# Logits in three fp32r passes, all query blocks per pair of heads, and probabilities scaled on GpSimd, in the sparse attention of a hybrid decoder layer

## The reference

```python
def block(args):                       # 128 queries each; here the kernel has its own blocks
    idx_logits = jnp.einsum('bqhd,bsd->bqhs', iqb, ik) * (IDX_HD ** -0.5)
    score = jnp.einsum('bqh,bqhs->bqs', iwb, jax.nn.relu(idx_logits))
    score = jnp.where(visible[None], score, -jnp.inf)
    _, idx = lax.top_k(score, k_sel)   # k_sel = 128 keys of 528
    ks, vs = k[idx], v[idx]
    logits = jnp.einsum('bqhd,bqkhd->bhqk', qb, ks) * (DSA_HD ** -0.5)
    logits = jnp.where(valid[:, None], logits, -jnp.inf)
    p = jax.nn.softmax(logits, axis=-1)
    return jnp.einsum('bhqk,bqkhd->bqhd', p, vs)
```

## Time and profile before

| | |
|---|---|
| median of 3 runs | 1045.75 us (1045.68 to 1053.85) |
| profiled execution: span, first to last instruction | 1044.6 us (no time of its own beside the span is given) |
| the runs' median above that span | 1.15 us |
| TensorE busy | 1033.1 us, 99% |
| VectorE busy | 782.0 us, 75% |
| GpSimd busy | 659.5 us, 63% |
| ScalarE busy | 471.6 us, 45% |
| granted TensorE clock, mean | 0.997 |
| instructions | 20236 |

### The profile page before, as it was taken

The page is one execution under the profiler, slowest core; times in us unless marked ns, Lnnn a source line. Parts: engine busy times, 40 slices in busy tenths (PEclk is TensorE's granted clock), DMA queues, the critical chain, the costliest instruction groups (busy, mean ns, idle before and its releaser), DMA issues.

```text
span 1044.6 us, 20236 instructions
## 1 busy us (share of the span) xinstructions
PE 1033.1 (99%) x7723; PEld 958.0 (92%) x7723; DVE 782.0 (75%) x1271; ACT 471.6 (45%) x766; POOL 659.5 (63%) x751
## 2 busy tenths in 40 slices
PE   9999999999999999999999999999999999999997
PEld 8999999999999999889878787778899999999997
DVE  7647897677676588699875584578999977777835
ACT  6433444334343354562455527444444443443335
POOL 6956787787686367269821304456887877866840
PEclk9999999999999999999999999999999999999999
DMA  7333342333432444345311102222333434334322
GB/s 209 101 98 97 97 112 82 112 96 97 111 94 80 122 118 116 83 117 149 90 33 41 42 21 63 79 71 81 84 101 103 122 107 112 101 92 111 92 61 81
DMA packets 178403, 98.73 MB, mean 95 GB/s; under 512 B 6787, under 2 KB 175798, under 8 KB 178310
## 3 DMA queue, kind: packets, MB, share of 16 engines
q1 hardware_dynamic: 178208, 97.38, 33.3%
q10 hardware_dynamic: 102, 0.08, 0.0%
HBM read 91.18 MB, written 2.10 MB: 89 GB/s over the span
## 4 chain that ended last, share of the span: by engine, by line
PE 93%; DVE 2%; ACT 1%; issue 1%; POOL 1%; DMA 1%; SPq 0%; DVEq 0%; ACTq 0%; POOLq 0%
PE ps L2542 44%; PE ps L2762 34%; PE ps L610 4%; PE ps L2578 2%; PE ps L799 1%; PE ps L748 1%; PE ps L778 1%; PE ps L916 1%; DMA xin<-in_x 1%; PE ps L957 0%; POOL wl L1852 0%; PE ps L691 0%; DVE mask L1404 0%; PE ps L811 0%; PE ps L595 0%
## 5 line engine op out<-in xcount | busy, mean ns | idle before, releaser
L1852 POOL TENSOR_TENSOR wl<-raw,wh 128x256 fp32r<-128x256 f32 x292 | 250.5, 892 | 198.6 <-ACT wh L1981 162.6
L1852 POOL TENSOR_TENSOR wxl<-raw,wxh 128x256 fp32r<-128x256 f32 x240 | 231.3, 989 | 140.5 <-ACT wxh L1981 140.0
L2542 PE MATMUL ps<-ah,wxh 128*128 128x264 f32 (+2 forms) x464 | 123.2, 319 | 0.3 <-POOL wxl L1852 0.3
L2542 PE MATMUL ps<-ah,wxl 128*128 128x264 f32 (+2 forms) x464 | 123.0, 318 | 0.0
L2542 PE MATMUL ps<-al,wxh 128*128 128x264 f32 (+2 forms) x464 | 122.8, 318 | 0.0
L2542 PE MATMUL ps<-xh,wh 128*128 128x264 f32 (+3 forms) x432 | 121.6, 333 | 0.2 <-DVE pja L1498 0.2
L2542 PE MATMUL ps<-xh,wl 128*128 128x264 f32 (+3 forms) x432 | 117.5, 323 | 0.0
L2542 PE MATMUL ps<-xl,wh 128*128 128x264 f32 (+3 forms) x432 | 117.4, 323 | 0.0
L2762 PE MATMUL ps<-xh,wh 128*128 128x264 f32 (+1 forms) x360 | 102.0, 283 | 0.0
L2762 PE MATMUL ps<-xl,wh 128*128 128x264 f32 (+1 forms) x360 | 101.9, 283 | 0.0
L2762 PE MATMUL ps<-xh,wl 128*128 128x264 f32 (+1 forms) x360 | 101.5, 282 | 0.0
(11 more groups left out here) (324 smaller groups left out, 2935.0 us busy)
## 6 DMA issues: line engine op xcount, KB each, us to landing
raw<-in_ffn_w_gate SPq DMA_DIRECT2D x44, 512.0 KB, 4.1
raw<-in_ffn_w_up SPq DMA_DIRECT2D x44, 512.0 KB, 4.1
raw<-in_ffn_w_down SPq DMA_DIRECT2D x80, 256.0 KB, 2.8
raw<-in_w_in SPq DMA_DIRECT2D x28, 512.0 KB, 4.3
raw<-in_w_out SPq DMA_DIRECT2D x8, 512.0 KB, 3.4
xin<-in_x SPq DMA_DIRECT2D x4, 512.0 KB, 5.7
raw<-in_ffn_w_down SPq DMA_DIRECT2D x16, 128.0 KB, 2.2
out<-xin SPq DMA_DIRECT2D x4, 512.0 KB, 3.5
```

The costliest lines, as they stand in the source:

```text
L1852: op = pool.tensor_tensor(dst[:, part], src[:, part], high[:, part].bitcast(F32), ALU.subtract)
L2542: mm = pe.matmul(ps[0:m, bank + a, 0:width], places(lo, PLACE[u], -(-WIDTH[u] // HALF_UNIT))[:, k * P:k * P + m], r[:, tile, t:t + width], ...
```

## The change

- **Order of the steps.** `att_step` now takes one pair of heads over all five blocks, then the next pair: pairs 0 to 4 are heads 0 and 1 with blocks 4, 3, 2, 1, 0, pairs 5 to 9 heads 2 and 3, and so on. A bank (2 or 3 in turn) holds one pair of heads for all queries, 512 columns.
- **Logits in three passes.** Queries and keys of a pair of heads get high parts (`qk_high`, ScalarE, into `qkh`) and low parts (`qk_low`, VectorE, into `pjl`, the place of `pjb` itself), twice two operations of up to 528 columns for each of four pairs of heads. `logits(p)` issues six fp32r matmuls in place of two float32 ones, the two heads by turns within each pass. The first and second pair's parts are made ahead of the loop, the others inside it. The 16 last keys are now made for two heads at a time in front of and behind the logits of block 4, three passes each.
- **Logits two pairs ahead.** The loop on TensorE and VectorE runs from -2; `lg` has six rows (`lg_more`), `pt` four buffers; `kdx` has its own tile instead of a part of `mask`. The two pairs' fill steps ahead of the loop's end are replaced by steps of the third gate unit, which is thereby finished ahead of `level(0)`.
- **Probabilities scaled before they are turned.** `invert_sums(p)` is a reciprocal of two columns for each pair on VectorE (20 in place of 5); GpSimd multiplies the probabilities by it (`scale_probs`, 40 operations on 100 or 112 partitions and all keys of the block), and `turn_probs` waits for that. `spread_sums`, `keep_spread` and `scale_out` are gone; `out_hi` and `out_lo` read PSUM, four times instead of five.
- **GpSimd's queue.** The low parts of four weight units, before in one piece each as soon as the high parts were there, are now sixteen quarters behind the scalings of pairs 2 to 17.
- The scratch space for dynamic transfers is set to 512.

```diff
+            QK_PASSES = ((0, 0), (0, 1), (1, 0))
+
             def logits(p):
+                b, hd0, s, w = att_step(2 * p)
+                j = hd0 // 2
+                if b == ATT_ORDER[0]:
+                    pe.wait_ge(qk_lo, 2 * (j + 1))
+                    if j >= 2:
+                        pe.wait_ge(m_lo, j - 1)
+                    elif j == 0:
+                        pe.wait_ge(v_out, V_OUT_ALL)
+                    tail(j, 0)
+                for c, (q_low, k_low) in enumerate(QK_PASSES):
+                    for e in range(2):
+                        rows = slice(HD * e, HD * (e + 1))
+                        mm = pe.matmul(ps[0:w, qk_bank(2 * p + e), 0:main_keys(b)], qk_operand(j, 0, q_low)[rows, s:s + w],
+                                       qk_operand(j, 1, k_low)[rows, 0:main_keys(b)], start=(c == 0), stop=(c == 2))
+                        if c == 2:
+                            mm.then_inc(qk_done, 1)
+                if b == ATT_ORDER[0]:
+                    pe.wait_ge(tail_done, 2 * j + 1)
+                    tail(j, 1)
...
-            def turn_probs(n, t):
+            def turn_probs(n):
                 b, hd, s, w = att_step(n)
-                pe.wait_ge(exp_done, n + 1)
+                pe.wait_ge(p_scaled, n + 1)
...
-            def spread_sums(i, t):
...
+            for p in range(-2, PAIRS):
+                if p + 2 < PAIRS:
+                    if p + 2:
+                        pe.wait_ge(lg_done, 2 * p + 4)
+                    logits(p + 2)
+                if p > 0:
                     values(p - 1)
+                if p < PAIRS - 2:
+                    fill_step(KT + 2 * (p + 2))
+                    fill_step(KT + 2 * (p + 2) + 1)
+                else:
+                    if p == PAIRS - 2:
+                        pe.wait_ge(lg_done, N_ATT)
+                    gate_steps(2, 2 * (p - PAIRS + 2), 2 * (p - PAIRS + 3))
+                if p >= 0:
+                    turn_probs(2 * p)
+                    turn_probs(2 * p + 1)
+            gate_steps(2, 4, 6)
             values(PAIRS - 1)
-            spread_sums(len(BLK) - 1, len(TURNS) - 1)
-            gate_steps(2, 2, 4)
+            gate_steps(2, 6, KT)
...
             level(0)
-            gate_steps(2, 4, KT)
             turn_kd(0)
...
-            b = ATT_ORDER[n // HEADS]
-            return (b, n % HEADS) + BLK[b]
+            j, i = divmod(n // 2, len(BLK))
+            b = ATT_ORDER[i]
+            return (b, 2 * j + n % 2) + BLK[b]
...
+            def qk_high(j):
+
+                act.wait_ge(q_roped, HEADS // 2 + j + 1)
+                if j >= 2:
+                    act.wait_ge(qk_done, 2 * len(BLK) * (j - 1))
+                    act.wait_ge(tail_done, 2 * (j - 1))
+                for key in range(2):
+                    c = 0 if key else META
+                    act.activation(qk_operand(j, key, 0)[:, c:], pjb[:, (HEADS // 2) * key + j, c:],
+                                   ACT.Copy).then_inc(qk_hi, 1)
...
+            def invert_sums(p):
+
+                w, c = att_step(2 * p)[3], 2 * p % 8
+                dve.wait_ge(exp_done, 2 * p + 2)
+                dve.reciprocal(rinv[0:w, c:c + 2], psum_of[0:w, c:c + 2]).then_inc(sum_inv, 1)
+
+            def qk_low(j):
+
+                for key in range(2):
+                    c = 0 if key else META
+                    dve.wait_ge(qk_hi, 2 * j + key + 1)
+                    dve.tensor_tensor(qk_operand(j, key, 1)[:, c:], pjb[:, (HEADS // 2) * key + j, c:],
+                                      qk_operand(j, key, 0)[:, c:].bitcast(F32), ALU.subtract).then_inc(qk_lo, 1)
...
+            qk_low(0)
+            for p in range(-2, PAIRS):
+                if p % 4 == 2:
+                    keep_fill((p + 2) // 4)
+                if p + 2 < PAIRS:
+                    masked(2 * p + 4)
+                    masked(2 * p + 5)
+                if p == -2:
+                    qk_low(1)
+                if p < 0:
+                    if p == -1:
+                        invert_sums(0)
+                    continue
                 gate_work(2 * p)
                 gate_work(2 * p + 1)
                 keep_probs(dve, 2 * p)
+                if p in (5, 10):
+                    qk_low(p // 5 + 1)
+                if p + 1 < PAIRS:
+                    invert_sums(p + 1)
+                if p % 5 == 1 and p > 1:
+                    out_lo(p // 5 - 1)
...
-            for m in range(4):
-                lo(U_MIX + M_GR + m)
+            def scale_probs(n):
+                b, hd, s, w = att_step(n)
+                row = lg_row(n)[0:w, 0:SEEN[b]]
+                pool.wait_ge(sum_inv, n // 2 + 1)
+                pool.tensor_scalar(row, row, rinv[0:w, n % 8:n % 8 + 1], None, ALU.mult).then_inc(p_scaled, 1)
+
+            def lo_piece(u, c):
...
+            for p in range(PAIRS):
+                scale_probs(2 * p)
+                scale_probs(2 * p + 1)
+                if 2 <= p < 18:
+                    lo_piece(U_MIX + M_GR + (p - 2) // 4, (p - 2) % 4)
```

More of the change, by code:

```diff
@@ new lines, in logits, with tail @@
+                if b == ATT_ORDER[0]:
+                    pe.wait_ge(tail_done, 2 * j + 1)
+                    tail(j, 1)
+            def tail(j, e):
+                s, w = BLK[ATT_ORDER[0]]
+                rows = slice(HD * e, HD * (e + 1))
+                for c, (q_low, k_low) in enumerate(QK_PASSES):
+                    mm = pe.matmul(ps[0:w, pv_bank(j), tail_cols(e)], qk_operand(j, 0, q_low)[rows, s:s + w],
+                                   qk_operand(j, 1, k_low)[rows, 512:TOK], start=(c == 0), stop=(c == 2))
@@ L827, in pe_mixer @@
             pe.wait_ge(v_kept, 6)
-            logits(0)
             for k in range(KT):
@@ L1210, in act_mixer @@
                         probs(n + 2)
-                    if p > 4 and n % HEADS == 4:
-                        keep_spread(p // 4 - 1)
                     if n == 20:
@@ L1631, in dve_mixer @@
                 if g == 2:
-                    out_lo(last)
                     keep_fill(6)
```

223 lines of the change are left out of this document (70 added, 153 removed).

## The result

| | before | changed |
|---|---|---|
| median of 11 runs each, us | 1049.02 | 1056.07 (1052.16 to 1059.35) |
| profiled execution's span, us | 1044.6 | 1050.4 |
| TensorE busy, us | 1033.1 | 1029.9 |
| GpSimd busy, us | 659.5 | 707.0 |

The ratio is 1.0071 with a 95% interval of 1.0051 to 1.0091: slower, by 0.7%. The forecast was 1044.6 us with a range up to 1050.5.

A forecast was written before the change was run, and what follows sets the result against it. The prediction took TensorE, busy for 99% of the span, as the bound. Work -5.9, start waits +0.7, loop waits +2.7 and level 1 +1.4 gave -1.1 us: span 1043.5, time 1044.6 us, range 1040 to 1050.5.

The forecast's parts named there:

- What bounds the kernel: Attention: TensorE is busy nearly throughout, so its removed work is won unless what it then waits for is late.
- Work, -5.9 in the sum: TensorE in the attention: spread sums -4.1 us, logits -2.4, tails +0.6, together -5.9 us.
- The heads run at once: Logits: a pair's two heads overlap in fp32r; the rival that they don't gave 1051.3 us, 6%.
- narrow passes at the float32 rate: Rival on logits of widths 228 and 128: groups take 1.32 and 0.82 us, time 1048.0 us, 25%.
- the tails: Tiny matmuls for the last 16 keys: 1.8 us before, 24 at 0.1 or 2.4 after, costing 0.6 us.
- Start waits, +0.7: Start of the attention: TensorE waits 1.7 us instead of 1.0 for high and low parts and masks.
- Waits in the loop for copies and masks, +2.7: Attention loop: 2.0 us for copies out of PSUM, 1.4 as a guess, less 0.7 waited now.
- the guess: Attention loop: 1.4 us for gate work meeting the widest masks and later low parts ahead of a reciprocal on VectorE.
- The scale hidden: GpSimd's scale ahead of the transposes: 1.0 us for 528 columns, with a 2.2 us path hidden behind 2.9 of TensorE's work.
- The rival that the probabilities come late: Loop: a scale at 1.45 us, or VectorE held up by GpSimd, costs +4.5 us, giving 1049.1 us, 15%.
- Level 1, +1.4: Behind the loop: with half-steps moved ahead of level 0, TensorE waits 1.4 us for VectorE's take of level 0.

The follow-up runs named there:

- refined: The all four kernel with later low parts, first masks ahead of the first fill unit, and two GpSimd weight units after the mask steps: 1043.64 us, ratio 0.9962.
- GpSimd later: Changed kernel with GpSimd's low parts of the third and fourth weight unit held until VectorE's first two low parts are made: 1054.35 us, ratio 1.0081.
- narrow at 256: Changed kernel with the logits of the two narrow blocks (128 and 228 keys) made 256 columns wide: 1053.30 us, ratio 1.0063.
- no scaling: Changed kernel without GpSimd's 40 multiplications of the probabilities, transposes waiting for the exponential alone: 1048.25 us, ratio 1.0011.
- float32: Changed kernel with logits and tails in float32 again, without high and low parts of q and k: 1050.66 us, ratio 1.0036.
- fill between: Changed kernel with one of each pair's two fill steps put between logits and values on TensorE: 1060.08 us, ratio 1.0112.
- early reciprocal: Changed kernel with the next pair's reciprocal ahead of the gate work on VectorE: 1055.83 us, ratio 1.0084.
- before, steps moved: Kernel before with only the last four half-steps of the third gate unit moved ahead of level 0: 1052.98 us, ratio 1.0029.
- steps ahead: Changed kernel with two of the fourth gate unit's four steps put ahead of level 1: 1054.37 us, ratio 1.0064.
- all four: Changed kernel with fill step between logits and values, earlier reciprocal, two gate steps ahead of level 1, first head pair's logits in float32: 1049.17 us, ratio 1.0017.
- values first: The refined kernel with both fill steps behind the values again: 1047.40 us, ratio 0.9988.
- refined, float32: The refined kernel with all logits in float32, without high and low parts of q and k: 1047.52 us, ratio 0.9993.

## Why the prediction was wrong

From 508 to level 1 it had -1.1 us, measured is +6.4. Of the 7.5 between them 4.8 are waits, 1.7 the clock and 1.0 work. The level that the sum was put on was low too: the median rose to 1049.02 for the same kernel, and the 1.15 us between span and time came from different executions (in all runs with both, an execution's time is 1.7 to 2.4 us above its own span).

**What bounds the kernel.** Right: TensorE, with no cover left. The scale, taken for hidden, came out in full (3.1 in waits, 3.9 saved without it). The copies did not: refined with and without their 3.2 us of waits is 0.2 us apart, since what removed them cost as much.

**Work, -5.9 in the sum; measured -4.9.** L811 is gone. The groups were priced well: 0.74, 0.62, 0.50 and 0.48 predicted for 428 columns and less, 0.75, 0.62, 0.49 and 0.44 measured. The heads run at once, so that rival falls, and so does the one of narrow passes at the float32 rate, which were to take 1.32 and 0.82. The widest can only be seen with its tails: 1.13, where 0.85 and a quarter of 2.4, 1.45, were predicted; the tails were put too high. The price of the old narrow groups was too high too: 0.63 and 0.52, from starts in the kernel before, against 0.563 and 0.406 where nothing is waited for. By the starts of the groups logits and tails win 4x(0.35+0.14+0.11+0.07-0.03) = 2.6 us and not 1.8, and with L811 6.7 us went. By busy time it is 4.9. Part of the 1.8 between them is waiting that the rows count as work, since a wait is listed only from the modelled end of the matmul ahead (0.28 listed is 0.35 by the starts, 0.84-0.49); the rest I can't place.

**Start waits, +0.7; measured +2.9.** This step failed. It put the low parts at 0.70 each, which holds with GpSimd idle (1.31 for two), though the earlier trace rows showed what a busy GpSimd does; and it did not ask what GpSimd does from 514 to 521. They took 1.1 and 1.2, and the mask steps ahead of them 1.0 more than with GpSimd idle (1.70 against 0.72). That is 1.9 of the 3.4 us, shown by the run with GpSimd later, in which 1.5 remain; those are VectorE's queue, with TensorE done at 517.4 and not at 518.4 as the prediction had it.

**Waits in the loop for copies and masks, +2.7 (2.0 for copies, less 0.7, and 1.4 as a guess); measured +2.5 for copies.** For eight waits of 0.24 to 0.28, 2.1 us, the mechanism, the place and the size were right. The last two, 1.1 together, lie where the logits have run out, which the prediction didn't see. Of what the guess was for (gate work, later low parts) only a wait of 0.33 shows, at 554.55 for a scale behind low parts, counted below with the scale. That the totals agree is luck. No run has the old order of blocks with all else changed, so that the order brings these waits is read from the timelines.

**The scale hidden; measured 3.1 in waits, 3.9 in all.** This step failed on the term of 1.0 us. The range of 0.8 to 1.45 was drawn from a copy and a two-input operation; it takes 1.6 us at 528 columns. At 1.45 the text already had it late by 0.3. The rival that the probabilities come late, with 15%, is what happened at this link. Its price, 4.5 against 3.9 measured, is near by luck: it was worked out from 27 operations of VectorE held up, not from the scale's own length.

**Level 1, +1.4; measured +1.5.** Right, and seen alone in the kernel before.

**The clock, no term; measured 1.7 in the profiled execution.** This step was missing. Of the eleven executions of the changed kernel eight have a mean clock of 0.991 to 0.994, which is most of the 4 us between the profiled one (1052.16) and the median; in which stage it falls in them no trace shows. In the profiles the half clock comes near a wait:

| run | wait of TensorE, us, its end | half clock from, for us | near 450 |
|---|---|---|---|
| before | none over 0.5 | none | 451.6, 3.4 |
| changed | 3.4, 520.8; 1.5, 611.5 | 522.0, 3.4; none behind 611.5 | none |
| narrow at 256 | 3.4, 519.9; 1.5, 610.5 | 520.1, 3.4; 612.3, 3.4 | none |
| no scaling | 3.4, 519.8; 1.5, 606.6 | 519.9, 3.4; 608.6, 3.4 | none |
| float32 | 1.5, 609.5 | 610.2, 6.8 | 449.8, 6.8 |
| fill between | 1.6, 531.5; 1.5, 555.6; 1.5, 617.1 | 532.6, 3.4; 556.5, 3.4; 617.9, 6.8 | 450.7, 6.8 |
| early reciprocal | 1.7, 530.3; 0.8, 555.3; 1.5, 614.5 | 531.3, 6.8; 555.2, 3.4; 616.6, 3.4 | 449.4, 6.8 |
| before, steps moved | 1.5, 610.2 | 611.5, 3.4 | 451.0, 6.8 |
| steps ahead | 5.8, 525.3; none at level 1 | 524.7, 6.8 | 449.6, 6.8 |
| all four | 2.5, 548.8 | 548.3, 6.8 | none |
| values first | 3.6, 525.8 | 524.8, 6.8 | 449.7, 6.8 |
| GpSimd later | 1.5, 519.0; 1.5, 610.7 | none | none |
| refined | none over 0.9 | none | 450.6, 6.8 |
| refined, float32 | none over 0.7 | none | none |

GpSimd later, and level 1 in the changed kernel, show that a wait doesn't always bring it; no run without a wait of 1.5 us or more has it in this stage. But it comes behind shorter waits too: the last column stands behind a wait of 0.5 us for ScalarE in the index stage, which ends at 448 to 450 in all fourteen profiles and was touched by no edit; eight have a half clock behind it and six have none. That a wait in this stage costs clock is shown best by the kernel before with and without the moved steps (7 of 12 against 1 of 29 executions at 0.994 or lower). What else decides is open.

## What to carry to other kernels

Price a wait on TensorE at more than its length: 1.5 us of it cost 1.6 at the full clock, and 3.0 by the ratio of all executions (5.0 by the medians, which also move with the clock ahead of the stage). Compare profiles from a mark that no edit reaches: here they came to it up to 4.6 us apart. When two groups are timed from start to start, first ask whether the second waits for something else; then nothing done in the first is worth anything, in either direction. And for each new VectorE operation on an early path write down what GpSimd does in the same microseconds, and the other way round, before you take its time from a row with the other idle.

## What the runs showed of the hardware

- GpSimd's multiplication by a value per partition mostly takes 1.60 us for 528 columns, 1.35 for 428, 1.10 for 328, 0.85 for 228 and 0.60 for 128: 2.5 ns a column and 0.28 us besides, so 3 ns a column at 528. That is near its two-input subtraction (0.74 for 256) and over twice its copy (0.40 for 256). Some are longer, one of 528 columns 2.10.
- VectorE's two-input operations and its in-place mask step wait for GpSimd's: mask steps of 0.38 and 0.43 us became 0.83 and 0.95, low parts of 0.69 and 0.70 became 1.10 and 1.22, and in two of fourteen profiles a mask step of 0.8 became 8.8, in one of them until GpSimd paused for 0.08 us. The selection steps of 0.5 to 0.7 us around them (lines 1410 and 1414) kept their length beside the same GpSimd work, and so did the masks made from logits in PSUM (0.75). The Trainium skill (SBUF — State Buffer, "SBUF: two separate sides") calls the shared ports an exclusive lock that blocks the loser for the whole instruction; the trace agrees, and shows more: the loser got no turn through ten instructions of the other engine in a row.
- Behind a switch between kinds of matmul the first one of 512 columns takes 0.34 us to the next, later ones 0.23: 0.11 us a switch.
- Behind the same wait of 0.5 us in the index stage TensorE's clock is at half (1.2 GHz) for 3.4 us in one profile and for 6.8 us in seven, and stays full in the other six.
- Three fp32r passes against float32, for two heads on one half of the rows each, win 0.145 us at 428 columns and lose 0.03 at 128.
